# Dilated attention in an fp32 hybrid stack: tokens ordered by residue modulo 4 instead of modulo 2, two 64-key groups sharing one tile

## What is computed

```python
DIL_GROUPS = ((128, 1), (512, 4), (2048, 16))     # (window, dilation), 256 tokens, 16 heads of 64
k, v = apply_rotary(kv[:, :, 0]), kv[:, :, 1]     # kv = rmsnorm(x, kv_norm) @ w_kv, for 3 groups
q = apply_rotary(h @ w_q)                         # for 3 groups
for g, (window, dilation) in enumerate(DIL_GROUPS):
    s = q[g] @ k[g].T * 64 ** -0.5                # only keys with 0 <= distance <= window
    s = where(valid and distance % dilation == 0, s, -inf)
    m = max(s); p = exp(s - m); den = sum(p)
    o[g] = p @ v[g] / den; lse[g] = m + log(den)
out = sum_g softmax_g(lse)[g] * o[g]              # then @ w_o
```

## Time and profile before

| | |
|---|---|
| median of 3 runs | 1244.09 us (1244.06 to 1244.33) |
| span of the profiled execution, first to last instruction | 1242.4 us |
| TensorE matmul busy | 1230.6 us, 99% of the span |
| TensorE weight loads busy | 1105.9 us, 89% |
| VectorE busy | 807.9 us, 65% |
| ScalarE busy | 695.0 us, 56% |
| GpSimd busy | 144.4 us, 12% |
| dilated stage | about 398 to 682 us of the span |

### The profile page before, as it was taken

One profiled execution on the slowest core, in us unless ns is written; L12 is line 12 of the kernel. 1 busy time (PEld: TensorE's weight loads), 2 busy tenths in 40 slices (PEclk: granted clock), 3 DMA queues, 4 the chain that ended last, 5 costly groups with the idle time before them and its releaser, 6 DMA issues.

```text
span 1242.4 us, 19229 instructions
## 1 busy us (share of the span) xinstructions
PE 1230.6 (99%) x7514; PEld 1105.9 (89%) x7514; DVE 807.9 (65%) x1231; ACT 695.0 (56%) x1002; POOL 144.4 (12%) x178
## 2 busy tenths in 40 slices
PE   9999999999999999999999999999999999999997
PEld 8888888888888999999998888888999899999896
DVE  5666656767667566666666878677666666666564
ACT  6444345655555655555554766555576556566554
POOL 1000001200001000000000410430201410201500
PEclk9999999999999999999999999999999999999999
DMA  8544443755554644444443655545454453363331
GB/s 332 207 164 169 170 157 134 255 186 190 189 185 144 199 157 134 147 142 140 152 167 130 224 201 182 200 157 183 148 175 164 143 200 106 117 205 138 136 136 51
DMA packets 33846, 208.54 MB, mean 168 GB/s; under 512 B 3985, under 2 KB 4258, under 8 KB 16226
## 3 DMA queue, kind: packets, MB, share of 16 engines
q1 hardware_dynamic: 31986, 201.32, 46.9%
q0 software_dynamic: 1488, 5.78, 1.3%
q10 hardware_dynamic: 288, 0.27, 0.1%
HBM read 206.30 MB, written 1.05 MB: 167 GB/s over the span
## 4 chain that ended last, share of the span: by engine, by line
PE 94%; DVE 3%; ACT 2%; issue 1%; POOL 0%; DVEq 0%; ACTq 0%; POOLq 0%
PE pair L600 18%; PE pair L602 17%; PE pair L601 17%; PE pair L742 12%; PE pair L736 6%; PE bank L600 3%; PE bank L602 3%; PE bank L601 3%; PE bank L1037 1%; PE bank L1062 1%; PE bank L1045 1%; PE bank L855 1%; ACT whi L1484 1%; PE bank L1012 1%; DVE wlo L2013 1%
## 5 line engine op out<-in xcount | busy, mean ns | idle before, releaser
L2013 DVE TENSOR_TENSOR wlo<-raw,whi 128x2048 fp32r<-128x2048 f32 (+5 forms) x208 | 431.2, 2077 | 216.1 <-ACT whi L1484 215.3
L1484 ACT ACTIVATE whi<-raw 128x2048 fp32r<-128x2048 f32 (+5 forms) x208 | 361.7, 1742 | 184.1 <-PE pair L602 156.1
L600 PE MATMUL pair<-whi,bhi 128*128 128x384 f32 (+3 forms) x528 | 189.3, 359 | 1.9 <-DVE blo L2039 1.6
L602 PE MATMUL pair<-whi,blo 128*128 128x384 f32 (+3 forms) x528 | 183.7, 348 | 0.0
L601 PE MATMUL pair<-wlo,bhi 128*128 128x384 f32 (+3 forms) x528 | 183.7, 348 | 0.0
L600 PE MATMUL pair<-whi,ahl 128*128 128x384 f32 (+3 forms) x416 | 153.5, 369 | 0.8 <-DVE wlo L2013 0.8
L742 PE MATMUL pair<-ahl,whi 128*128 128x512 f32 x640 | 153.2, 391 | 0.0
L601 PE MATMUL pair<-wlo,ahl 128*128 128x384 f32 (+3 forms) x416 | 149.1, 358 | 0.0
L602 PE MATMUL pair<-whi,ahl 128*128 128x384 f32 (+3 forms) x416 | 149.1, 358 | 0.0
L742 PEld LDWEIGHTS pair<-ahl,whi 128*128 128x128 f32 x640 | 117.5, 188 | 22.6
L600 PEld LDWEIGHTS pair<-whi,bhi 128*128 128x128 f32 x528 | 100.9, 191 | 11.7 <-issue 2.9
(11 more groups left out here) (322 smaller groups left out, 1879.0 us busy)
## 6 DMA issues: line engine op xcount, KB each, us to landing
raw<-wstream_d SPq DMA_DIRECT2D x136, 1024.0 KB, 4.9
raw<-wstream_d SPq DMA_DIRECT2D x56, 768.0 KB, 4.2
raw<-wstream_d SPq DMA_DIRECT2D x4, 832.0 KB, 4.4
raw<-wstream_d SPq DMA_DIRECT2D x4, 800.0 KB, 4.8
gain_row<-rows_d POOLq DMA_DIRECT2D x5, 512.0 KB, 4.2
arena<-mem_d POOLq DMA_DIRECT2D x2, 1024.0 KB, 7.1
raw<-wstream_d SPq DMA_DIRECT2D x4, 384.0 KB, 3.2
raw<-wstream_d SPq DMA_DIRECT2D x4, 288.0 KB, 2.8
```

The source lines that it names most:

```text
L600: pe.matmul(out_ap, lhi, rhi, start=first, stop=False, skip_group_check=True)
L602: return pe.matmul(out_ap, llo, rhi, start=False, stop=last, skip_group_check=True)
L1484: act.activation(whi[:, n % RING, 0:width[n]], raw[:, n % RAW, 0:width[n]], ACT.Copy).then_inc(hi_ready, 1)
L2013: dve.tensor_tensor(wlo[:, n % RING, 0:width[n]], raw[:, n % RAW, 0:width[n]], whi[:, n % RING, 0:width[n]].bitcast(F32), ALU.subtract).th ...
```

## The change

The tokens of the stage are ordered by residue modulo 4 (`CLASSES` = 4 classes of `CLS` = 64 tokens): tile 0 holds residues 0 and 1, tile 1 residues 2 and 3. The order is now made once, where the activations are read out of PSUM at the head of the stage, so `tokens` reads its tiles contiguously. Groups 1 and 2 of a head are computed per class, 64 queries against 64 keys. Both results lie in one tile of 128 columns: for the first class of a tile as (group 1, group 2), for the second as (group 2, group 1), so that one product with a value tile whose rows hold group 1's values in one half and group 2's in the other sums both groups. A tile of scores is 384 wide instead of 512. ScalarE lays the values out for that, with 8 instructions over half of the partitions per pair instead of 2. Both tiles' scores of a head lie in one PSUM bank per tile.

```diff
-ORDER = (0, 2, 1)
+CLASSES = 2 * NT
+CLS = SEQ // CLASSES
-DIL_W = sum(DIL_KEYS)                      # 512
+DIL_W = SEQ + 2 * CLS                      # 384
+V_PLACES = tuple((h, g) for g in range(NG) for h in range(2))

+        def in_place(rows):
+            return rows.rearrange("p (r j) -> p r j", r=CLASSES)
+        def by_class(rows):
+            return rows.rearrange("p (j r) -> p r j", r=CLASSES)

@@ spread_phases: 4 matmuls of 64 weight columns become 8 of 32
-                for t in range(NT):
-                    rows = slice(t * P // NT, (t + 1) * P // NT)
-                    for f in range(NT):
-                        mm = pe.matmul(bank[rows, 0, f:f + 1], phase[:, :, f], x_rstd[:, t:t + 1], start=True, stop=True)
+                for t in range(NT):
+                    for c in range(2):
+                        for part in range(NT):
+                            rows = slice(c * CLS + part * CLS // NT, c * CLS + (part + 1) * CLS // NT)
+                            mm = pe.matmul(bank[rows, 0, t:t + 1], of_class[:, :, 2 * t + c], x_rstd[:, part:part + 1], start=True, stop=True,
+                                           tile_position=(0, rows.start))

@@ dil_scores
                 for qt in range(NT):
-                    for g in range(NG):
-                        i = PLACES.index((h, g))
-                        rows = slice((i % 2) * ATT_HD, (i % 2 + 1) * ATT_HD)
-                        nk = DIL_KEYS[g]
-                        k0 = 0 if nk == SEQ else qt * P
-                        mm = pe.matmul(flat[:, spot(g, qt):spot(g, qt) + nk], d_t[rows, 3 + i // 2, qt * P:(qt + 1) * P],
-                                       d_t[rows, i // 2, k0:k0 + nk], start=True, stop=True)
+                    i = PLACES.index((h, 0))
+                    rows = slice((i % 2) * ATT_HD, (i % 2 + 1) * ATT_HD)
+                    pe.matmul(flat[:, qt * 512:qt * 512 + SEQ], d_t[rows, 3 + i // 2, qt * P:(qt + 1) * P], d_t[rows, i // 2, :],
+                              start=True, stop=True)
+                    for side in range(2):
+                        for c in range(2):
+                            i = PLACES.index((h, ((1, 2), (2, 1))[c][side]))
+                            rows = slice((i % 2) * ATT_HD, (i % 2 + 1) * ATT_HD)
+                            own = slice(qt * P + c * CLS, qt * P + (c + 1) * CLS)
+                            at = qt * 512 + SEQ + side * CLS
+                            mm = pe.matmul(flat[c * CLS:(c + 1) * CLS, at:at + CLS], d_t[rows, 3 + i // 2, own], d_t[rows, i // 2, own],
+                                           start=True, stop=True)

@@ dil_pturn: 8 transposes become 6
-                for s in range(0, NT * DIL_W, P):
-                    mm = pe.transpose(dil_banks(n)[:, s:s + P], d_p[n % 2][:, s:s + P], ident[:, :])
+                for qt in range(NT):
+                    for s in range(0, DIL_W, P):
+                        mm = pe.transpose(dil_banks(n)[:, qt * 512 + s:qt * 512 + s + P], d_p[n % 2][:, qt * DIL_W + s:qt * DIL_W + s + P], ident[:, :])

@@ dil_mix: after the matmuls of group 0, which stay
+                for qt in range(NT):
+                    for c in range(2):
+                        for h in range(2):
+                            item = slice(P + c * P + h * ATT_HD, P + c * P + (h + 1) * ATT_HD)
+                            own = slice(qt * P + c * CLS, qt * P + (c + 1) * CLS)
+                            mm = pe.matmul(out_t[h][:, own], v[:, qt, item], pt[h][:, qt, SEQ + c * CLS:SEQ + (c + 1) * CLS], start=False,
+                                           stop=(qt, c) == (NT - 1, 1), skip_group_check=True)

@@ tokens of the stage: tile=by_phase is left out (in_order is the default)
-                tokens("a", bhi, blo, between=steps[4:8], tile=by_phase)
+                tokens("a", bhi, blo, between=steps[4:8])

@@ ScalarE, read of the activations (VectorE's low half likewise)
+                        if classes:
+                            o, rows = in_place(o), by_class(rows)

@@ ScalarE, read of the values
-                read_block(d_v[b % 2], PW, scale=ph_rstd)
+                read_values(d_v[b % 2])
+            def read_values(v):
+                p, n, _ = w.next_block("a")
+                low, high = slice(0, CLS), slice(CLS, P)
+                for t in range(NT):
+                    act.activation(v[low, t, 0:2 * P], pair[low, p, t, 0:2 * P], ACT.Copy, scale=ph_rstd[low, t:t + 1]).then_inc(act_step, 1)
+                    act.activation(v[high, t, :].rearrange("p (a d) -> p a d", a=3)[:, 0:3:2, :],
+                                   pair[high, p, t, 0:2 * P].rearrange("p (a d) -> p a d", a=2), ACT.Copy,
+                                   scale=ph_rstd[high, t:t + 1]).then_inc(act_step, 1)
+                    act.activation(v[high, t, P:2 * P], pair[low, p, t, 2 * P:3 * P], ACT.Copy, scale=ph_rstd[low, t:t + 1]).then_inc(act_step, 1)
+                    ins = act.activation(v[low, t, 2 * P:3 * P], pair[high, p, t, 2 * P:3 * P], ACT.Copy, scale=ph_rstd[high, t:t + 1])
+                    ins.then_inc(drained_a[p] if t == NT - 1 else act_step, 1)

@@ VectorE: dil_max in two instructions of 384 instead of four of 256; dil_pt copies 384 instead of 512
-                softmax_max(dil_banks(n), d_mask, d_p[n % 2], ((False, 0, slice(0, SEQ), slice(0, SEQ)), (False, 1, slice(SEQ, 512), slice(512, 512 + SEQ)),
-                             (True, 0, slice(512, 512 + SEQ), slice(SEQ, 512)), (True, 1, slice(512 + SEQ, 1024), slice(512 + SEQ, 1024))),
+                softmax_max(dil_banks(n), d_mask, d_p[n % 2], ((False, 0, slice(0, DIL_W), slice(0, DIL_W)), (False, 1, slice(512, 512 + DIL_W), slice(DIL_W, 2 * DIL_W))),
```

More of the change, by code:

```diff
@@ L156, in shape_tables, with mask @@
     ret = np.concatenate(decay + [cos, cos, sin, sin], axis=1)
-    place = np.concatenate([n[t::NT] for t in range(NT)])
+    classes = [[n[2 * t + c::CLASSES] for c in range(2)] for t in range(NT)]
+    place = np.concatenate([keys for halves in classes for keys in halves])
+    def mask(g, queries, keys):
+        window, dil = GROUPS[g]
+        dist = queries[:, None] - keys[None, :]
+        return np.where((dist >= 0) & (dist % dil == 0) & (dist <= window), f(0), f(NEG)).astype(f)
     masks = []
     for qt in range(NT):
[L161 to L165, removed]
+        masks.append(mask(0, place[qt * P:(qt + 1) * P], place))
+        masks.append(np.concatenate([np.concatenate([mask(g, own, own) for g in ((1, 2), (2, 1))[c]], axis=1)
+                                     for c, own in enumerate(classes[qt])], axis=0))
     inv = (f(500000.0) ** (-np.arange(0, ROPE_DIMS, 2, dtype=f) / f(ROPE_DIMS))).astype(f)
@@ L1086, in _ @@
                 if b == 0:
-                    first_tokens("a", held[0], by_phase)
+                    first_tokens("a", held[0])
                 else:
-                    tokens("a", bhi, blo, between=steps[0:4], tile=by_phase)
-                tokens("a", bhi, blo, between=steps[4:8], tile=by_phase)
+                    tokens("a", bhi, blo, between=steps[0:4])
+                tokens("a", bhi, blo, between=steps[4:8])
                 p = (w.block - 1) % 2
@@ L1094, in _ @@
                     pe.wait_ge(q_lo, KD)
-                tokens("a", ahi, alo, between=steps[8:12], tile=by_phase)
+                tokens("a", ahi, alo, between=steps[8:12])
             c = PAIRS - 1
@@ L1527, in post_squares, with turn_out @@
                         act.activation(scratch[:, t, nb, :], sums[:, nb, :], ACT.Square, accum_out=sq_sum[:, i:i + 1]).then_inc(ssq_ready, 1)
-            def turn_out(dst, tiles, gain, src=None, each=False):
+            def turn_out(dst, tiles, gain, src=None, each=False, classes=False):
                 g = w.up("turn") - 1
@@ L1539, in turn_out, with rows_out @@
                 mm.then_inc(turned_hi, 1)
-            def rows_out(dst, gain, each=False):
+            def rows_out(dst, gain, each=False, classes=False):
                 for g in range(KD // 2):
-                    turn_out(dst, (2 * g, 2 * g + 1), gain, bank[:, g, :], each)
+                    turn_out(dst, (2 * g, 2 * g + 1), gain, bank[:, g, :], each, classes)
             def read_block(dst, cs=None, func=ACT.Copy, scale=None):
@@ L2039, in low_half, with turn_out @@
                 return dve.scalar_tensor_tensor(lo, src, cols[:, gcol:gcol + 1], hi.bitcast(F32), ALU.mult, ALU.subtract)
-            def turn_out(dst, tiles, gain, src, each=False):
+            def turn_out(dst, tiles, gain, src, each=False, classes=False):
                 dve.wait_ge(turned_hi, w.up("turn"))
```

55 lines of the change are left out of this document (25 added, 30 removed).

## The result

| | before | after |
|---|---|---|
| median, us | 1244.15 (1244.06 to 1244.33, 4 runs) | 1261.46 (1260.23 to 1261.62, 4 runs) |
| ratio to before | | 1.0135, 95% interval 1.0123 to 1.0147 |
| span of the profiled execution | 1242.4 | 1259.8 |

The forecast was 1252.4 (1244.5 to 1259.0). The direction was right, the size was not, and the time lies above the range. First two parts of the profile's page after, answering to the earlier trace rows: busy time, and the chain by engine.

What follows compares the result with a forecast made beforehand. TensorE, busy 99% of the span, was taken as the bound: scores +14.9, transposes -3.5, value product -3.1, sum +8.3 us, giving 1252.4 us; range 1244.5 to 1259.0.

Steps and rivals of the forecast that it cites:

- the reading by distances: TensorE's queue: a step's cost is read from distances between instruction starts; scores 1.29 us before, 2.22 forecast after.
- Term 3: Scores on TensorE: five shape switches per head instead of two, quarters no longer beside group 0; +0.93 per head, +14.9 us.
- The nearest row: Value product before the change: going from 128x64 to 128x128 weights was paid, 1.89 us against 1.74 by widths.
- free passage: Rival, scores: switching between 64x128 and 64x64 weights costs nothing, leaving only gains, -6.6 us, 1237.5; chance 14%.
- shared bank: Rival, scores: no drain, but row halves writing one PSUM bank take turns; +7.2, net +0.6, 1244.7 us; chance 6%.
- The step that failed: ScalarE's eight value reads: 2.4 us instead of 0.93, its copy ready 0.3 us before head 1's scores, cost 0.
- The rival with this mechanism: ScalarE's value reads stall head 1's scores, or the quarters' weights show; up to 6.5 us, about 1256 to 1259; chance 12%.
- the prices of the prediction: Scores on TensorE: a shape switch costs 0.20 us into 128 weight columns, 0.14 us into 64.

Runs made afterwards that it cites:

- grouped: pt_first with both group 0 score matmuls (64x128 weights) first, then all eight of 64x64, three switches per head instead of five: 1247.13 us, ratio 1.0026.
- pt_first: The changed kernel with ScalarE's copy of head 0's transposed probabilities ahead of its eight value reads instead of behind them: 1252.39 us, ratio 1.0066.
- two_banks: pt_first with the scores' PSUM banks as before the change: group 0 of both tiles in the first, 64x64 results in the second: 1252.44 us, ratio 1.0070.
- all_quarters: two_banks with each group 0 score matmul of 64x128 weights cut into two of 64x64, so all score matmuls share one shape: 1236.10 us, ratio 0.9934.
- reads_by_half: The changed kernel with ScalarE's eight value reads sorted by source and target half of the partitions: 1257.75 us, ratio 1.0102.
- late_scores: The changed kernel with the scores of head 1 hung in at step 10 instead of 9: 1252.96 us, ratio 1.0078.
- quarters_long_wait: all_quarters with the value reads ahead of the copy again and four more 64x128 reads per pair before them: 1254.71 us, ratio 1.0092.

## Why the prediction was wrong, point by point

- **What bounds the kernel, and the reading by distances:** right. All step prices came out within 0.03 us: the scores at 2.20 (2.22), the transposes at 0.66 (0.66), the value product at 1.47 (about 1.5).
- **Term 3, five switches per head:** right. With five switches a head inserts 2.21 us, with three 1.87, and with two and everything in one shape 1.21. The cleanest of the three is grouped, where nothing but the order changed: 0.34 for two switches, as priced. The nearest row, where only the weight columns change, was the right one to go by. The Trainium skill, TensorEngine Tiling (Array Packing), Key Properties, says that a change of the tiling mode drains the array; by that rule grouped must gain over pt_first and two_banks must not. So it came: 5.3 us less, and 1252.44 beside 1252.39.
- **The rivals "free passage" and "shared bank":** both refuted, by the changed kernel and by two_banks. Whether two row halves in one shape could share a bank at the same time was not tried.
- **The step that failed:** "start to start I estimate 0.36 at 256 and 0.25 at 128, so eight take 2.4 us [...] 0.3 us are left: 0". They took 3.5, and the wait put at 0 came to 5.9 us. I had carried over the overlap of two reads over 128 partitions to reads that change the half of the partitions each time, which no row showed. The rival with this mechanism and its price stood in the text (6.5 us at most, measured 5.9), with a chance of 12%. With a margin of 0.3 us against an error of 1.1 it should have been the likeliest case, or near it: 1252.4 + 5.9 = 1258.3.
- **What no case had:** the half clock, put at nothing without a reason. It took 3.1 us, which carried the time out of the range. Why it came in these places is only partly known. The rows gave a clock of 1.00 throughout, and I asked nowhere what waits and emptied arrays would do to it.
- Without those two the sum stands: pt_first took 1252.39 us against the 1252.4 of the forecast.

## What to carry to other kernels

Cutting a matmul into smaller ones saved nothing here, because the shape of the weights then changed back and forth: two changes cost 0.34 us, and cutting the large matmul to the small shape too (more instructions, one shape) turned +0.7% into -0.6%. When an engine that "has room" gets its work in more pieces, don't check its load alone, but the one hand-over that TensorE waits for, and put what TensorE needs first ahead of what it needs later: two exchanged lines were worth 9 us. A margin of 0.3 us, computed with an overlap that the new form of the instruction has not shown, is no margin.

## What the runs showed of the hardware

- Neighbouring reads of PSUM by ScalarE overlapped by some 0.1 us if both used the same partitions at source and target (128 partitions, or the same halves: two of 64x256 in 0.81 us). If the source half changed, alone or together with the target half, the next started about 25 ns after the end of the one before. A target half that changes alone did not occur. This is not the whole rule. A read of the lower half behind an instruction over 128 partitions overlapped too (445.80 behind 444.40 + 1.49). And the weight split behind `dil_pt` starts 24 ns after its end (449.83), though both use all 128 partitions; why stays open.
- In all_quarters, group 0 streamed 256-wide through both column halves of one row half, with the sixteen 64-wide records of a head beside it in the other. A head inserts 1.21 us; less two switches (0.34 by the prices of the prediction) that leaves 0.87, where the estimate for group 0 alone is 0.86.
- The granted clock fell to its lower level for stretches of a few microseconds after idle time of 0.72 us followed by scores of 2.2 us. It also fell without a wait: at the back-to-back scores of the last pair in reads_by_half, and where the scores stood twice in a row (1302.05 us against the 1284.5 that the pieces give). Products then took 0.32 instead of 0.174 us. Which executions of a kernel it hits varied: 1252.61 to 1256.07 for late_scores, 1252.85 to 1257.82 for quarters_long_wait. What exactly decides it stays open.
